# Two transformer blocks in one kernel: the first two query blocks of a head pair share one attention step

## The reference, cut to what matters

```python
s = jnp.einsum('bqgrd,bqgkld->bgrqkl', qc, ksel) * scale      # selected branch
p = masked_softmax(s, m_sel, (-2, -1))
o_sel = jnp.einsum('bgrqkl,bqgkld->bqgrd', p.astype(vsel.dtype), vsel)
...
s = jnp.einsum('bqgrd,bkgd->bgrqk', qc, kwc) * scale          # windowed branch
p = masked_softmax(s, m_win, -1)
o_win = jnp.einsum('bgrqk,bkgd->bqgrd', p.astype(vwc.dtype), vwc)
return gc[..., 0:1] * o_cmp + gc[..., 1:2] * o_sel + gc[..., 2:3] * o_win
```

```python
s = jnp.einsum('bqhd,bkhd->bhqk', qc, kc).astype(jnp.float32) * scale + bias
p = jax.nn.softmax(s, axis=-1).astype(v.dtype)
return jnp.einsum('bhqk,bkhd->bqhd', p, vc)
```

## Time and profile before

| | |
|---|---|
| three runs | 1675.2, 1679.76 and 1680.8 us, median 1679.76 us |
| the profiled execution | 1675.47 us; span from the first to the last instruction 1673.7 us |
| TensorE busy | 1594.5 us, 95% of the span |
| VectorE, ScalarE, GpSimd busy | 931.7, 579.7, 201.5 us |
| first attention, first scores to next stage | 204.28 to 331.66 us |
| second attention, first scores to next stage | 1129.39 to 1204.05 us |

### The profile page before, as it was taken

How to read it: one execution, slowest core, us unless ns; L and a number is a source line. 1 busy time by engine, 2 the same in 40 slices (tenths; PEclk the granted TensorE clock), 3 DMA queues, 4 the chain that set the end, 5 groups by cost and what they waited for, 6 DMA issues and landing times.

```text
span 1673.7 us, 21655 instructions
## 1 busy us (share of the span) xinstructions
PE 1594.5 (95%) x7872; PEld 1273.4 (76%) x7872; DVE 931.7 (56%) x1466; ACT 579.7 (35%) x910; POOL 201.5 (12%) x107
## 2 busy tenths in 40 slices
PE   6997899899999999999999999999899999999997
PEld 4875656688888888887776789776688787777885
DVE  5147466565666665334753843335465777777323
ACT  4231355543433333223225222335444323222221
POOL 3453211100000000000002353131100000000000
PEclk9998999999999999999999999999999999999998
DMA  5421111152232223232222211162152222223231
GB/s 220 160 95 63 57 59 50 58 189 89 101 100 90 98 90 117 87 103 76 92 101 95 76 51 57 39 226 70 70 188 88 89 100 92 96 88 119 87 104 68
DMA packets 49847, 163.12 MB, mean 97 GB/s; under 512 B 5089, under 2 KB 5353, under 8 KB 49649
## 3 DMA queue, kind: packets, MB, share of 16 engines
q1 hardware_dynamic: 46544, 156.09, 27.1%
q10 hardware_dynamic: 3232, 6.08, 1.1%
HBM read 148.50 MB, written 13.65 MB: 97 GB/s over the span
## 4 chain that ended last, share of the span: by engine, by line
PE 82%; DVE 9%; issue 4%; ACT 3%; POOL 0%; DVEq 0%; DMA 0%; ACTq 0%
PE banks L1466 24%; PE banks L1468 23%; PE banks L1467 23%; PE banks L1557 2%; PE banks L1583 2%; PE banks L1566 1%; PE banks L1787 1%; PE banks L1776 1%; PE banks L1640 1%; ACT at_pt L786 1%; PE banks L1771 1%; ACT at_p L777 1%; DVE w_lo L502 1%; DVE t_raw L1011 1%; DVE at_sm L1112 1%
## 5 line engine op out<-in xcount | busy, mean ns | idle before, releaser
L1466 PE MATMUL banks<-h_hi,w_hi 128*128 128x512 f32 x1312 | 533.9, 407 | 33.9 <-POOL w_lo L502 14.1
L1468 PE MATMUL banks<-h_hi,w_lo 128*128 128x512 f32 x1312 | 514.0, 392 | 0.0
L1467 PE MATMUL banks<-h_lo,w_hi 128*128 128x512 f32 x1312 | 513.4, 391 | 0.0
L678 ACT ACTIVATE w_hi<-w_raw 128x1024 fp32r<-128x1024 f32 (+1 forms) x228 | 251.5, 1103 | 447.3 <-PE banks L1468 409.7
L1466 PEld LDWEIGHTS banks<-h_hi,w_hi 128*128 128x128 f32 x1312 | 247.7, 189 | 103.8 <-issue 33.0
L1468 PEld LDWEIGHTS banks<-h_hi,w_lo 128*128 128x128 f32 x1312 | 247.3, 189 | 53.2
L1467 PEld LDWEIGHTS banks<-h_lo,w_hi 128*128 128x128 f32 x1312 | 247.9, 189 | 51.6 <-issue 4.8
L502 DVE TENSOR_TENSOR w_lo<-w_raw,w_hi 128x1024 fp32r<-128x1024 f32 (+1 forms) x167 | 216.7, 1298 | 79.1 <-ACT w_hi L678 79.1
L502 POOL TENSOR_TENSOR w_lo<-w_raw,w_hi 128x1024 fp32r<-128x1024 f32 x61 | 148.9, 2442 | 422.1 <-ACT w_hi L678 422.1
L1466 PE MATMUL banks<-act_hi,w_hi 128*128 128x512 f32 x352 | 137.3, 390 | 1.6 <-DVE t_val L1011 0.8
L1467 PE MATMUL banks<-act_lo,w_hi 128*128 128x512 f32 x352 | 137.1, 389 | 0.0
(11 more groups left out here) (274 smaller groups left out, 1927.8 us busy)
## 6 DMA issues: line engine op xcount, KB each, us to landing
w_raw<-in_w_up SPq DMA_DIRECT2D x88, 512.0 KB, 3.4
w_raw<-in_w_fill SPq DMA_DIRECT2D x44, 512.0 KB, 3.5
w_raw<-in_w_down SPq DMA_DIRECT2D x32, 704.0 KB, 4.0
late_scratch<-stage SPq DMA_DIRECT2D x44, 256.0 KB, 2.0
w_raw<-in_w_mix SPq DMA_DIRECT2D x16, 512.0 KB, 4.4
sg<-late_scratch SPq DMA_DIRECT2D x16, 512.0 KB, 3.8
w_raw<-in_w_out SPq DMA_DIRECT2D x16, 512.0 KB, 3.5
w_raw<-in_w_in SPq DMA_DIRECT2D x15, 512.0 KB, 3.5
```

The lines of the kernel that those rows point to most:

```text
L678: act.activation(w_hi[:, c.slot, 0:kt * P], w_raw[:, c.slot, 0:kt * P], ACT.Copy)\
L1466: pe.matmul(dst, w_h, hi[:, kr, :], start=first and n == 0, stop=False)
L1467: pe.matmul(dst, w_h, lo[:, kr, :], start=False, stop=False)
L1468: mm = pe.matmul(dst, w_l, hi[:, kr, :], start=False, stop=last and n == len(ks) - 1)
```

## The change

Query blocks 0 and 1 of a head pair, with scores of 128 and 256 columns, now share a step: the scores of block 0 go to columns 0 to 127 of the score bank and those of block 1 to columns 128 to 383. A head pair takes three steps (384, 384 and 512 columns) instead of four; the first attention has 24 steps and the second 12. Query blocks keep their own maxima, sums and biases, so the masks, exponentials and scalings are still issued per query block and half. Shift, inversion, copies of the transposed weights, and semaphores between engines are per step. The table spreads the same 30 and 22 pieces over 24 and 12 steps. The small buffers of maxima, sums and inverses are 24 columns instead of 12.

```diff
-                            ("unit", 16, 22, 16)])
+                            ("unit", 12, 22, 12)])
...
-                            ("unit", 32, 30, 32)])
+                            ("unit", 24, 30, 24)])
...
+            def members(self, s):
+
+                return [(m, i, m * P, (i + 1) * P) for m, i in enumerate(self.pairs[s][1])]
+
+            def half_done(self, s, half):
+
+                return self.at[s] + (half + 1) * len(self.pairs[s][1]) if s >= 0 else 0
+
+            def width(self, s):
+                return sum((i + 1) * P for i in self.pairs[s][1])
...
+        BLOCKS = ((0, 1), (2,), (3,))
+        att1 = Attention(1, [(j, blocks, b) for j in range(4) for blocks in BLOCKS for b in range(2)],
+                         2 * len(BLOCKS), at1_sm, at1_p, at1_pt, cols1, o1_hi, o1_lo)
+        att2 = Attention(2, [(j, blocks, 0) for j in range(4) for blocks in BLOCKS],
+                         len(BLOCKS), at2_sm, at2_p, at2_pt, cols2, ob_hi, ob_lo)
...
                         for half in range(2):
-                            c = 2 * (s % 2) + half
                             wait(act, a.flipped, 2 * (s - 2) + half + 1 if s >= 2 else 0)
-                            act.activation(a.p[:, s % 2, half, 0:w], a.sm[:, half, 0:w], ACT.Exp,
-                                           bias=a.nbias[:, c:c + 1], scale=DH ** -0.5,
-                                           accum_out=a.sums[:, c:c + 1]).then_inc(a.exped, 1)
+                            for m, i, off, w in a.members(s):
+                                c = 4 * (s % 2) + 2 * m + half
+                                act.activation(a.p[:, s % 2, half, off:off + w], a.sm[:, half, off:off + w], ACT.Exp,
+                                               bias=a.nbias[:, c:c + 1], scale=DH ** -0.5,
+                                               accum_out=a.sums[:, c:c + 1]).then_inc(a.exped, 1)
...
                             dve.wait_ge(a.scored, 2 * s + half + 1)
-                            wait(dve, a.exped, 2 * (s - 1) + half + 1 if s else 0)
-                            dve.tensor_tensor_reduce(a.sm[:, half, 0:w], banks[:, BS + half, 0:w],
-                                                     mask(j, half, w), 1.0, NEG, ALU.add, ALU.max,
-                                                     a.nbias[:, c:c + 1]).then_inc(a.masked, 1)
-                        dve.wait_ge(a.masked, 2 * s + 2)
+                            wait(dve, a.exped, a.half_done(s - 1, half))
+                            for m, i, off, w in a.members(s):
+                                c = 4 * (s % 2) + 2 * m + half
+                                dve.tensor_tensor_reduce(a.sm[:, half, off:off + w], banks[:, BS + half, off:off + w],
+                                                         mask(j, half, w), 1.0, NEG, ALU.add, ALU.max,
+                                                         a.nbias[:, c:c + 1]).then_inc(a.masked, 1)
+                        dve.wait_ge(a.masked, a.at[s + 1])
...
-                        for half in range(2):
-                            wait(pe, a.masked, 2 * (s - 1) + half + 1 if s else 0)
-                            pe.matmul(banks[:, BS + half, 0:(i + 1) * P], q_tile(j)[rows(half), i * P:(i + 1) * P],
-                                      k_tile(j, b)[rows(half), 0:(i + 1) * P], start=True, stop=True)\
-                                .then_inc(a.scored, 1)
+                        j, blocks, b = a.pairs[s]
+                        for m, i, off, w in a.members(s):
+                            for half in range(2):
+                                if m == 0:
+                                    wait(pe, a.masked, a.half_done(s - 1, half))
+                                mm = pe.matmul(banks[:, BS + half, off:off + w], q_tile(j)[rows(half), i * P:(i + 1) * P],
+                                               k_tile(j, b)[rows(half), 0:w], start=True, stop=True)
+                                if m == len(blocks) - 1:
+                                    mm.then_inc(a.scored, 1)
...
-                            for k in range(i + 1):
+                            for k in range(a.width(u) // P):
                                 mm = turn(banks[:, BT + half, k * P:(k + 1) * P],
                                           a.p[:, u % 2, half, k * P:(k + 1) * P])
```

More of the change, by code:

```diff
@@ L422, in __init__ @@
                 self.pairs, self.per_tile = pairs, per_tile
+                self.at = [0]
+                for _, blocks, _ in pairs:
+                    self.at.append(self.at[-1] + 2 * len(blocks))
                 self.sm, self.p, self.pt, self.o_hi, self.o_lo = sm, p, pt, o_hi, o_lo
-                self.nbias, self.sums, self.inv = cols[:, 0:4], cols[:, 4:8], cols[:, 8:12]
+                self.nbias, self.sums, self.inv = cols[:, 0:8], cols[:, 8:16], cols[:, 16:24]
                 self.scored = sem(f"scored{b}")
@@ L435, in __init__, with columns @@
                 self.low = sem(f"o_low{b}")
-        att1 = Attention(1, [(j, i, b) for j in range(4) for i in range(NT) for b in range(2)],
-                         2 * NT, at1_sm, at1_p, at1_pt, cols1, o1_hi, o1_lo)
-        att2 = Attention(2, [(j, i, 0) for j in range(4) for i in range(NT)],
-                         NT, at2_sm, at2_p, at2_pt, cols2, ob_hi, ob_lo)
+            def members(self, s):
[4 more added lines that the diff above has]
+                return sum((i + 1) * P for i in self.pairs[s][1])
+            def columns(self, s):
+                return slice(4 * (s % 2), 4 * (s % 2) + 2 * len(self.pairs[s][1]))
+        BLOCKS = ((0, 1), (2,), (3,))
[3 more added lines that the diff above has]
+                         len(BLOCKS), at2_sm, at2_p, at2_pt, cols2, ob_hi, ob_lo)
         d_pe, d_dve, d_act = sem("d_pe"), sem("d_dve"), sem("d_act")
@@ L1104, in attention @@
                     if s < n:
[L1105 to L1107 removed]
+                        j = a.pairs[s][0]
                         for half in range(2):
[L1109 removed]
                             dve.wait_ge(a.scored, 2 * s + half + 1)
[L1111 to L1114 removed]
@@ L1118, in attention @@
+                        dve.wait_ge(a.masked, a.at[s + 1])
+                        dve.tensor_scalar(a.nbias[:, a.columns(s)], a.nbias[:, a.columns(s)], -DH ** -0.5, None,
+                                          ALU.mult).then_inc(a.shifted, 1)
                     u = s - 1
                     if 0 <= u < n:
-                        j, i, b = a.pairs[u]
-                        two = slice(2 * (u % 2), 2 * (u % 2) + 2)
-                        dve.wait_ge(a.exped, 2 * u + 2)
-                        dve.reciprocal(a.inv[:, two], a.sums[:, two]).then_inc(a.inverted, 1)
+                        j, _, b = a.pairs[u]
@@ L1134, in attention @@
-                            ins.then_inc(a.weighted, 1)
+                            for m, i, off, w in a.members(u):
+                                c = 4 * (u % 2) + 2 * m + half
+                                pr = a.p[:, u % 2, half, off:off + w]
+                                g = (j + 4 * half) * 3 + 1 + b
+                                if gated_:
+                                    ins = dve.tensor_scalar(pr, pr, a.inv[:, c:c + 1], gate_t[:, i, g:g + 1],
+                                                            ALU.mult, ALU.mult)
+                                else:
+                                    ins = dve.tensor_scalar(pr, pr, a.inv[:, c:c + 1], None, ALU.mult)
+                                ins.then_inc(a.weighted, 1)
@@ L1580, in attention @@
                         end = u % a.per_tile == a.per_tile - 1 if first_values else True
-                        for k in range(i + 1):
-                            for half in range(2):
-                                mm = pe.matmul(banks[rows(half), BO + j % 2, i * P:(i + 1) * P], v_tile(j, b, half, k),
-                                               a.pt[:, half, k * P:(k + 1) * P],
-                                               start=opens and k == 0, stop=end and k == i)
+                        for m, i, off, w in a.members(u):
+                            for k in range(i + 1):
+                                for half in range(2):
+                                    mm = pe.matmul(banks[rows(half), BO + j % 2, i * P:(i + 1) * P],
+                                                   v_tile(j, b, half, k), a.pt[:, half, off + k * P:off + (k + 1) * P],
+                                                   start=opens and k == 0, stop=end and k == i)
                         mm.then_inc(a.summed, 1)
@@ L1588, in attention @@
                     if 0 <= u < n:
-                        j, i, b = a.pairs[u]
                         for half in range(2):
-                            pe.wait_ge(a.weighted, 2 * u + half + 1)
+                            pe.wait_ge(a.weighted, a.half_done(u, half))
                             wait(pe, a.fetched, 2 * (u - 1) + half + 1 if u else 0)
-                            for k in range(i + 1):
```

(1 more changed line is left out.)

26 lines of the change are left out of this document (6 added, 20 removed).

## The result

The changed kernel takes 1668.62 us (median of 11 runs, 1665.67 to 1673.37) against 1677.02 us for the kernel before (median of 11 runs, 1675.2 to 1682.29). The ratio is 0.9946 with a 95% interval of 0.9933 to 0.996: faster by 0.54%, 8.4 us between the medians. The profiled execution took 1665.67 us, its span is 1663.9 us.

The account below looks back on a forecast made before the run. TensorE was taken to bound the kernel, its attention waits being for ScalarE's copies. Savings of 5.6 us (second attention) and 3.4 us (first) made 9.0 us, giving 1666.5 or 1670.8 by starting point; forecast 1669 us, range 1661 to 1678.

Parts of the forecast that it names:

- Which stage gains: Both attentions: the second stage loses 5.6 us and the first 3.4 us, 9.0 us together.
- Second attention, waits: Second attention: TensorE's waits fall from 7.4 to 3.2 us, with no wait behind a 512 step.
- The 1.0 us kept for GpSimd's splits: Second attention: 1.0 us of waits allowed for five splits meeting 0.6 to 1.7 us of spare; bounds 0 and 8.
- The step on where the pieces lie: Second attention: 512 steps with one filling piece lacked 1.1 us of cover; with two, cover 5.6 exceeds chain 4.2.
- The merged scores: Both attentions: scores of blocks 0 and 1 cost 0.42 + 0.63 us in one step as in two.
- the bound of 2.5: Merged scores, both attentions: further overlap of four matmuls could save 0.21 us twelve times, up to 2.5 us; none taken.
- First attention, irregular waits: First attention: waits from pair ends and GpSimd's splits total 5.0 us, 3.5 before plus 1.5; bounds 0 and 15.
- half price: Shift on VectorE, kernel before: held 2.19 us under GpSimd's split, it cost TensorE a 1.10 us wait.
- The lack of 0.5 us in four merged steps: First attention: chain 4.8 us against cover 4.3 us in four merged steps, 2.0 us of waits in all.
- the first attention getting worse: Rival, chance 0.25: splits cost full 2.2 us at merged steps, irregular waits 8.8 us; total 4.4 us less, 1673.
- Waits did not go in both: Rival, chance 0.15: first attention's irregular waits fall to 1.5 us, half the scores overlap comes; 13.7 us less, 1664.
- The loop over `at_sm`: Rival, chance 0.08: one buffer per half puts merged steps' masks in a row with TensorE; 8 us more, 1686 at most.

Follow-up runs that it names:

- e1: Changed kernel with only the second attention merging blocks 0 and 1, the first kept at 32 steps: 1668.84 us, ratio 0.9946 to the kernel before.
- e2: Changed kernel with only the first attention merging blocks 0 and 1, the second kept at 16 steps: 1679.5 us, ratio 1.001 to the kernel before.
- e4: Kernel before, unmerged, with the second attention's 22 filling pieces laid out so every 512 step has two: 1675.01 us, ratio 0.9971.
- e10: Kernel before, unmerged, with the shift on ScalarE in both attentions and two pieces at every 512 step of the second: 1668.11 us, ratio 0.9941.
- e3: Changed kernel with the four-column shift moved from VectorE to ScalarE, ahead of the exponentials, in both attentions: 1662.47 us, ratio 0.9899 to the kernel before.
- e7: Changed kernel with the merged step's score matmuls issued half by half instead of block by block: 1667.4 us, ratio 0.9939 to the kernel before.
- e5: Changed kernel with two filling pieces behind each merged step of the first attention from the second head pair on: 1664.0 us, ratio 0.9907 to before.
- e8: Changed kernel with the first attention's chunk splits made by VectorE instead of GpSimd: 1659.28 us, ratio 0.9884 to the kernel before.
- e6: Changed kernel with the shift on ScalarE and two filling pieces behind the first attention's merged steps from the second pair on: 1661.1 us, ratio 0.9898 to before.

## Why the prediction was right, and where it was not

1669 us was predicted and 1668.62 measured; 9.0 us less in two stages, and 8.3 found in the profile. Its parts do not fit as well as the sum does. In the first attention 3.2 us more of waits and 1.7 us of clock stood against 2.3 us less of scores and 0.8 us less of waits in the second; that these nearly cancel was luck. (They leave 7.2 us. Of the 1.1 us to 8.3, 0.6 are idle time that none of these waits holds, and 0.4 more work that went.)

- **Which stage gains: right in kind.** The second attention was to fall by 5.6 us and the first by 3.4; they fell by 7.3 and 1.0. By e1 and e2 all that can be measured of the whole comes from the second.
- **Second attention, waits: right, some too high.** 3.2 us predicted, 2.4 measured, and none behind a 512 step. The 1.0 us kept for GpSimd's splits was not needed: the spare of merged steps with two pieces took them up. The longest hold of a merged step's shift there, 1.62 us at 1141.52, is followed by a wait of 0.17 us. The step on where the pieces lie is confirmed by e4: 2.4 us come from the layout alone.
- **The merged scores: mis-sized.** The step "Scores of blocks 0 and 1 cost 0.42 + 0.63 in one step as in two" is wrong by 0.19 us: they take 0.86, no more than scores of 384 columns were reckoned at (0.84). Twelve times 0.19 is 2.3 us, next to the bound of 2.5 that I named and took none of. With it the work that goes is 2.5 + 8 x 0.19 = 4.0 us in the first and 1.4 + 4 x 0.19 = 2.2 in the second; e10 against e3 measures 4.15 and 1.9, and after against before 2.3 in the second. That the four matmuls in a row overlap is read from the pitch; e7 shows only that their order does not matter.
- **First attention, irregular waits: mis-sized, and the step that failed most.** I took 5.0 us for them, 1.5 more than before, and 8.6 for all waits; 11.8 were measured. I had seen that three splits run while the shift of a merged step is due, but took a blocked shift at the half price that it had before (1.10 us of wait for 2.19 of blocking). Two of the three held it; the third came no sooner than the shift (298.62). In a merged step chain and cover are about equal, by that same working 4.8 and 4.3 us, so a block passes nearly in full: the waits are 2.15 us for a shift of 2.18 and 1.92 for one of 2.40, and 0.29 at the same two places without the block (e3). At half price these two would have cost some 2.2 us instead of 4.1. What else I missed is the held scaling at the start, 2.08 us (before, 1.62), and the ends of pairs, up to 1.38 us. The lack of 0.5 us in four merged steps, 2.0 us in the sum, shows only as 0.29 us in each of the other two. I counted seven splits in this stage; there are eight. e3, e5 and e8 each take the two long waits away by another means (another engine for the shift, more cover and other places for the splits, no split on GpSimd), and each brings the stage to 120.5 to 120.8 us. e3 leaves the split where it was, and e7 has both in place, the shift just not late enough to be held: these two make the blocked shift the cause and not the length of the chain alone. The Trainium skill (Advanced Engine Details and Errata, VectorE Performance Modes) says that GpSimd and VectorE's instructions in two-port modes block each other. The shift and scaling rows agree, and e8, without a split on GpSimd, has no such row.
- **First attention, the clock: not in the prediction.** 1.7 us went to a granted clock of 0.56 over 3.91 us behind the longest wait, in after, e2 and e7 alike; e7 has a second such stretch of 1.6 us.
- **The rivals.** The first one, the first attention getting worse, was right in its mechanism and near in size: 8.6 + 3.8 + 0.8 = 13.2 us of waits, against 11.8 of waits and 1.7 of clock. The total came out as forecast all the same, because the scores gave 2.3 us and the second attention's waits 0.8 more than reckoned. Waits did not go in both. The loop over `at_sm` did not decide: VectorE's masks waited for exponentials 0.7 us in all in the first attention and 1.5 in the second, and these 1.5 at its start, where TensorE waited for nothing. The three versions without the two long waits reach 0.988 to 0.991.

What stays open: why e8 and e6, 2.7 us apart in the first attention, have medians 1.8 us apart the other way. Their profiled executions have the order of the stage (1660.07 and 1657.65 us); the other executions of e6 reach up to 1663.83, and the intervals overlap. Nor do the stages make up all of the medians: e8's two are 13.9 us shorter than before, its median is 19.0 us lower. Between the attentions, where no edit changes TensorE's work, the twelve profiles have 796.2 to 800.5 us.

## What to carry to other kernels

Merging two steps puts the chains of both behind one wait: where chain and cover come out about equal, a stall that was half hidden passes nearly in full, so price each known stall again at full length in the merged steps. A tiny instruction that everything waits for (here four columns, 0.17 us) should not be on the engine that another one's long instruction can hold; moving it, or the long one, was worth 5.6 to 5.9 us here, 1.7 of them clock, more than the merge itself brought in that stage. Read busy time with suspicion where an instruction's mean is far above its shortest: part of it is waiting that no wait row shows.

## What the hardware did that I had not expected

- A 128x4 instruction of VectorE took 2.18 and 2.40 us instead of 0.17, ending each time with GpSimd's instruction (within 0.03 us). Where both started in the same hundredth, it took 0.17 us (298.62, and 270.31 in e7). Masks that read PSUM kept their length under a split, and the inversion did too (128x2, 0.16 us at 232.86 in e3, the split from 232.76).
- One wait of TensorE of 2.15 us was followed, 1 us after work came back, by 3.91 us at a granted clock of 0.56, and in the kernel of e2 by the same 3.91 us at 0.56 (237.80 to 241.71). The waits of 2.08 us at 212.52 and of 1.92 us at 274.39 in the same stage had no such stretch behind them: the windows 212.52:236.97 and 274.39:281.00 have a clock of 1.00. In e7 a wait of only 1.39 us was followed at once by 3.12 us at 0.50. So the length of the wait alone does not decide it; what does I did not find out.
- The scores of two query blocks, fp32 with 64 rows, both halves, take 0.86 us in a row where they take 0.42 + 0.63 in two places.
